# The output projection's second half of the last four tiles in a second PSUM bank, and five dead probability rows lent to the gathers of U

## What is computed

```
def diff_attention(q, k, v, lam, lambda_init, subln_g):
    ...
        p = jax.nn.softmax(sc, axis=-1)
        w = p[:, :, 0] - lam * p[:, :, 1]
...
        mix = jnp.einsum('bsk,kd->bsd', jnp.concatenate([att, ssd], axis=-1), w_out[l])
        x = layer_norm(alpha * x + mix, ln1_g[l], ln1_b[l])
        ffn = peer_ffn(x, peer_wq[l], peer_keys[l], peer_u[l], peer_v[l])
        x = layer_norm(alpha * x + ffn, ln2_g[l], ln2_b[l])
...
    def apply(args):
        hx, idx, g = args
        act = jax.nn.gelu(jnp.einsum('td,tkd->tk', hx, u_tab[idx]), approximate=False) * g
        return jnp.einsum('tk,tkd->td', act, v_tab[idx])
```

## Time and profile before

| | us |
|---|---|
| median of 3 executions | 3350.33 (3341.79, 3350.33, 3350.97) |
| the profiled execution, its own time | 3342.97 |
| its span in the profile | 3341.0 |
| PE busy | 2794.2 (84%) |
| DVE busy | 1888.3 (57%) |
| POOL busy | 1495.0 (45%) |
| ACT busy | 596.5 (18%) |

### The profile page before, as it was taken

The page is one execution under the profiler, slowest core; times in us unless marked ns, Lnnn a source line. Parts: engine busy times, 40 slices in busy tenths (PEclk is TensorE's granted clock), DMA queues, the critical chain, the costliest instruction groups (busy, mean ns, idle before and its releaser), DMA issues.

```text
span 3341.0 us, 32682 instructions
## 1 busy us (share of the span) xinstructions
PE 2794.2 (84%) x10171; PEld 1378.1 (41%) x10171; DVE 1888.3 (57%) x4634; ACT 596.5 (18%) x1288; POOL 1495.0 (45%) x1348
## 2 busy tenths in 40 slices
PE   8999979654255888747679999999999999999996
PEld 3455445432122555524334444444444444444442
DVE  3335444787589778768855555545565544445113
ACT  1321143221002778700000000100000000000000
POOL 0010011344444433444475566666666566665552
PEclk9999979887577989778889999999999999999998
DMA  3000021455688999899899999999999999999995
GB/s 129 28 26 26 26 81 60 142 173 177 214 309 284 349 375 384 326 373 336 315 386 388 402 398 398 370 406 389 404 403 379 377 398 396 406 396 381 367 371 204
DMA packets 307579, 981.57 MB, mean 294 GB/s; under 512 B 29904, under 2 KB 57680, under 8 KB 306640
## 3 DMA queue, kind: packets, MB, share of 16 engines
q0 software_dynamic: 184320, 671.17, 52.8%
q1 hardware_dynamic: 120464, 307.85, 24.4%
q10 hardware_dynamic: 2624, 0.46, 0.1%
HBM read 941.63 MB, written 37.75 MB: 293 GB/s over the span
## 4 chain that ended last, share of the span: by engine, by line
PE 28%; issue 13%; POOL 12%; DMA 9%; DVE 4%; ACT 3%; ACTq 1%; DVEq 0%; another core or an unknown queue 0%; POOLq 0%
PE part L1771 9%; PE hid L1752 8%; POOL u_ring L1690 8%; DMA v_ring<-in_peer_v_dram,ids_t 7%; PE acc L1809 6%; POOL v_ring L1704 4%; PE turn_ps L1744 4%; DVE u_ring L2087 2%; ACT dense_sums L1849 1%; PE part L1780 1%; DMA u_ring<-in_peer_u_dram,ids_u 1%; ACTq L1850 1%; ACT dense_sums L1851 1%; DMA room<-in_peer_v_dram 1%; ACT room L1897 1%
## 5 line engine op out<-in xcount | busy, mean ns | idle before, releaser
L2087 DVE CUSTOM_DVE_ANT_0 u_ring<-u_ring,x_rows_in 128x1024 f32<-128x1024 f32 x560 | 676.4, 1223 | 510.9 <-DMA u_ring<-in_peer_u_dram,ids_u 458.1
L1690 POOL DMA_INDIRECT u_ring<-in_peer_u_dram,ids_u x560 | 640.7, 1144 | 480.1 <-DVE dots L2087 328.9
L1704 POOL DMA_INDIRECT v_ring<-in_peer_v_dram,ids_t x560 | 595.4, 1063 | 484.9 <-PE acc L1809 318.2
L1771 PE MATMUL part<-room 128*128 128x512 f32 x1536 | 692.9, 601 | 87.9 <-DVE room L2063 77.5
L1752 PE MATMUL hid<-x1t_dense,room 128*128 128x384 f32 x2048 | 699.4, 495 | 4.6 <-DMA room<-in_peer_ut_dram 3.1
L1752 PEld LDWEIGHTS hid<-x1t_dense,room 128*128 128x128 f32 x2048 | 385.3, 192 | 338.1 <-issue 100.4
L1771 PEld LDWEIGHTS part<-room 128*128 128x128 f32 x1536 | 291.8, 192 | 447.8 <-issue 337.5
L1809 PE MATMUL acc<-v_ring,line 128*32 128x512 f32 x2240 | 296.2, 650 | 68.5 <-DMA v_ring<-in_peer_v_dram,ids_t 64.1
L1887 ACT ACTIVATE room<-hid 128x384 f32<-128x384 f32 x128 | 62.8, 491 | 1462.0 <-PE hid L1752 1224.4
L2073 DVE TENSOR_TENSOR dense_sums<-dense_sums,part 128x512 f32<-128x512 f32 x186 | 125.5, 684 | 262.9 <-PE part L1771 230.0
L412 PE MATMUL bank<-w_ring,xt 128*128 128x512 f32 x512 | 226.8, 596 | 2.6 <-issue 2.6
(11 more groups left out here) (318 smaller groups left out, 2657.2 us busy)
## 6 DMA issues: line engine op xcount, KB each, us to landing
wq_pair<-in_peer_wq_dram SPq DMA_DIRECT2D x32, 2048.0 KB
room<-in_peer_ut_dram SPq DMA_DIRECT2D x128, 512.0 KB
room<-in_peer_v_dram SPq DMA_DIRECT2D x128, 512.0 KB
gate_grid<-room SPq DMA_DIRECT2D x6, 4096.0 KB, 13.8
room<-gate_grid SPq DMA_DIRECT2D x32, 768.0 KB
w_ring<-in_w_in_dram SPq DMA_DIRECT2D x5, 2048.0 KB, 7.9
u_ring<-in_peer_u_dram,ids_u POOLq DMA_INDIRECT x560
v_ring<-in_peer_v_dram,ids_t POOLq DMA_INDIRECT x560
```

The costliest lines, as they stand in the source:

```text
L1690: pool.indirect_dma_start(u_ring[:, n % U_RING, :], None, peer_u, bass.IndirectOffsetOnAxis(ap=ids_u[:, q, k:k + 1], axis=0))\
L1704: pool.indirect_dma_start(row, None, peer_v, bass.IndirectOffsetOnAxis(ap=ids_t[:, q % 2, token:token + 1], axis=0))\
L1771: last = mm.matmul(part[k % 3][:], weights[:, n % 2, i, d * P:(d + 1) * P], vd[:, slot, half * 512:(half + 1) * 512], start=(i == 0), stop ...
L2087: vec.tensor_tensor_reduce(u_ring[:, n % U_RING, :], u_ring[:, n % U_RING, :], x1[:, q % 2, :], 1.0, 0.0, ALU.mult, ALU.add, dots[:, q % 2 ...
```

## The change

Two edits. The second half of the output projection of tiles t = 4 to 7 is accumulated in `TP[1]` instead of `OP`, and its bank is claimed and released through `t_free[1]` instead of `op_free`. And from k = `SPARE_FROM` = 48 on the gathers of U go round a ring of nine rows: the three rows of `probs0`, the two of `probs1` and the four of `u_rows`. Five new semaphores say that they landed; `spare_free`, given by ACT once it has seen the last item transposed (step 33), lets POOL issue k = 48 to 52. At step 33 POOL issues the gathers of steps 34 and 35, and later always those of two steps ahead. Eight semaphores of the scan and `spare_free` are released at the end of `build_mixer`, so that other numbers are handed out in `build_experts`.

```diff
+        SPARE_FROM = 4 * (items + 2 - CHOICE - 7)
+
+        def second_bank(t):
+
+            return TP[1] if t >= 4 else OP
...
+        def row_at(k):
+
+            if k < SPARE_FROM:
+                return u_rows[:, k % U_FIRST_RING, :]
+            i = (k - SPARE_FROM) % 9
+            return probs0[:, i, :] if i < 3 else probs1[:, i - 3, :] if i < 5 else u_rows[:, i - 5, :]
...
+        def rows_asked(n):
+
+            if n <= items:
+                return products(n + 1)
+            return [k for i in ((n + 1, n + 2) if n == items + 1 else (n + 2,)) for k in products(i)]
...
-                    for k in products(n + 1):
+                    for k in rows_asked(n):
                         if k % TOPK == 0:
                             pool.wait_ge(ids_ready, 1).then_inc(ids_ready, -1)
-                        pool.wait_ge(rows_free, 1).then_inc(rows_free, -1)
-                        pool.indirect_dma_start(u_rows[:, k % U_FIRST_RING, :], None, peer_u,
+                        if SPARE_FROM <= k < SPARE_FROM + 5:
+                            pool.wait_ge(spare_free, 1).then_inc(spare_free, -1)
+                        else:
+                            pool.wait_ge(rows_free, 1).then_inc(rows_free, -1)
+                        pool.indirect_dma_start(row_at(k), None, peer_u,
...
+                            elif half and t >= 4:
+                                pe.wait_ge(t_free[1], 1).then_inc(t_free[1], -1)
                             else:
                                 pe.wait_ge(op_free, 1).then_inc(op_free, -1)
+                            out = second_bank(t) if half else OP
                             for c in range(KC):
-                                last = mm.matmul(OP[:], mix_t[:, c, :], w_ring[:, half, c, :],
+                                last = mm.matmul(out[:], mix_t[:, c, :], w_ring[:, half, c, :],
...
+                        if m == items - 1:
+                            act.sem_inc(spare_free, 5)
...
-                            vec.scalar_tensor_tensor(out=part, in0=part, scalar=ALPHA, in1=OP[:],
+                            out = second_bank(t) if half else OP
+                            vec.scalar_tensor_tensor(out=part, in0=part, scalar=ALPHA, in1=out[:],
                                                      op0=ALU.mult, op1=ALU.add)
-                            dve.drain().then_inc(op_free, 1)
+                            dve.drain().then_inc(t_free[1] if half and t >= 4 else op_free, 1)
```

More of the change, by code:

```diff
@@ L209, in build_mixer @@
         xbc_smooth = sem("xbc_smooth")
-        dt_by_heads = sem("dt_by_heads")
-        dt_copied = sem("dt_copied")
-        dt_done = sem("dt_done")
+        dt_by_heads = handshake("dt_by_heads")
+        dt_copied = handshake("dt_copied")
+        dt_done = handshake("dt_done")
         xbc_ready = sem("xbc_ready")
@@ L215, in build_mixer @@
         conv_free = sem("conv_free")
-        turns_ready = sem("turns_ready")
+        turns_ready = handshake("turns_ready")
         trig_ready = sem("trig_ready")
-        lam_ready = sem("lam_ready")
-        lam_exped = sem("lam_exped")
+        lam_ready = handshake("lam_ready")
+        lam_exped = handshake("lam_exped")
         roped_ready = sem("roped_ready")
@@ L761, in build_mixer @@
         rows_landed = [sem(f"rows_landed{i}") for i in range(U_FIRST_RING)]
+        rows_landed += [sem(f"spare_landed{i}") for i in range(5)]
+        spare_free = handshake("spare_free")
         rows_free = sem("rows_free")
@@ L826, in products, with landed @@
             return range(min(done, FIRST_SLOTS), min(done + count(n), FIRST_SLOTS))
+        def row_at(k):
[3 more added lines that the diff above has]
+            return probs0[:, i, :] if i < 3 else probs1[:, i - 3, :] if i < 5 else u_rows[:, i - 5, :]
+        def landed(k):
+            if k < SPARE_FROM:
+                return k % U_FIRST_RING
+            return (U_FIRST_RING + (k - SPARE_FROM) % 9) if (k - SPARE_FROM) % 9 < 5 else (k - SPARE_FROM) % 9 - 5
+        def rows_asked(n):
+            if n <= items:
+                return products(n + 1)
+            return [k for i in ((n + 1, n + 2) if n == items + 1 else (n + 2,)) for k in products(i)]
         def tail(n, lag):
@@ L889, in _ @@
                             pool.tensor_copy(x1_first[:], tile).then_inc(x1_first_ready, 1)
-                    for k in products(n + 1):
+                    for k in rows_asked(n):
                         if k % TOPK == 0:
                             pool.wait_ge(ids_ready, 1).then_inc(ids_ready, -1)
-                        pool.wait_ge(rows_free, 1).then_inc(rows_free, -1)
-                        pool.indirect_dma_start(u_rows[:, k % U_FIRST_RING, :], None, peer_u,
+                        if SPARE_FROM <= k < SPARE_FROM + 5:
[3 more added lines that the diff above has]
+                        pool.indirect_dma_start(row_at(k), None, peer_u,
                                                 bass.IndirectOffsetOnAxis(ap=ids_first[:, k:k + 1], axis=0))\
-                            .then_inc(rows_landed[k % U_FIRST_RING], 16)
+                            .then_inc(rows_landed[landed(k)], 16)
             @block.tensor
@@ L1138, in _ @@
                             dve.wait_ge(x1_first_ready, 1)
-                        slot = k % U_FIRST_RING
-                        dve.wait_ge(rows_landed[slot], (k // U_FIRST_RING + 1) * 16)
-                        vec.tensor_tensor_reduce(u_rows[:, slot, :], u_rows[:, slot, :], x1_first[:], 1.0, 0.0, ALU.mult, ALU.add,
+                        row = row_at(k)
+                        dve.wait_ge(rows_landed[landed(k)], 16 * sum(landed(i) == landed(k) for i in range(k + 1)))
+                        vec.tensor_tensor_reduce(row, row, x1_first[:], 1.0, 0.0, ALU.mult, ALU.add,
                                                  dots_first[:, k:k + 1]).then_inc(rows_free, 1)
```

## The result

The changed kernel took 3316.65 us (median of four executions, 3300.18 to 3319.16) against 3350.01 before: ratio 0.9897, 95% interval 0.9876 to 0.9917. Its profiled execution took 3315.28 with a span of 3313.3, against 3341.0 before; that is 27.7 us less, with 30.5 foretold.

The account below looks back on a forecast made before the run. The attention block's last stretch was taken as a chain of waits with no engine full. 28.4 + 2.1 = 30.5 us gave 3312.5 or 3319.8, so 3316 was forecast; range 3308 to 3324 (71%).

Parts of the forecast that it names:

- Steps 26 and 30: Output projection: PE's waits of 1.09 and 1.02 us between the halves go with the second bank, saving 2.1 us.
- Step 34: Projection's second half follows the first without pause; DVE's second addition starts at 819.2 instead of 827.70, saving 8.5 us.
- The first round of gathers: k = 48 to 55 are issued by about 820, so rows for steps 34 and 35 land before DVE asks.
- POOL is not held at `spare_free`: ACT's last copy fulfils the wait with 17 us of cover; the rival that POOL is held had 1%.
- To the last tile's projection: Work on x1, transposes and `att` move up; the last projection starts at 842.2, 9.5 us earlier.
- the 0 for POOL's port: DVE dot products beside POOL's work on x1 could delay L884 by 0 to 2.3 us; the sum took 0.
- Step 38, the halves back to back: Last projection takes 9.49 + 7.11 us, DVE waiting about 7; 19.6 us saved up to here, step 34's 8.5 included.
- Steps 38 to 41: 10.3 us from second addition to step 39 unchanged; last twelve dot products end about 883.7, 28.4 us earlier.
- The tail keeps its pace: Rival, 15%: DMA engines limit the gathers, twelve dot products again take 23 us; gain 21.7 us, time 3321 to 3329.
- Lost behind the barrier: Rival, 8%: the expert part meets its transfers in another phase and loses 20 to 30 us; time 3333 to 3355.
- slower by the clock: Rival, 4%: PE's granted clock in the expert part is 0.02 lower, losing 40 us; time 3355 to 3365.
- Two levels of the time of before: Four executions before were read as two levels, the timed median 7.4 us above the profiled one; forecast set between them.

## Why the prediction was right, step by step

I had 3316 us, and 3316.65 was measured. The mechanism held; the sum was short by 2.3 in the block (30.5 for 32.8), and the agreement to 1 us of the median is luck, since the four executions lie between 3300.18 and 3319.16 and the expert part alone scatters by 8.

- *Steps 26 and 30*, 2.1: 1.8 by the kernel that takes just these back, 1.7 between the kernel before (793.84 - 683.55 = 110.3) and the changed one (108.6). Right but for the clock at step 30: the waits went, and the matmuls took 16.45 us in place of 8.80 + 7.11.
- *Step 34*, 8.5: the additions are 10.08 - 1.41 = 8.7 us nearer. Right.
- *The first round of gathers; POOL is not held at `spare_free`.* Right. POOL issues `probs` behind the last `u_rows` with no wait of its own, 17 us after ACT's last copy:

```profile
807.41 0.94 POOL L923 DMA_INDIRECT u_rows<-in_peer_u_dram,ids_first  x1 [0.31 <-issue]
808.65 0.94 POOL L923 DMA_INDIRECT probs<-in_peer_u_dram,ids_first  x1 [0.30 <-issue]
```

- *To the last tile's projection*, 48.4 us from the start of step 34's: 48.0 (843.07 - 795.10). Right, the 0 for POOL's port included, though the meeting did take place: one dot product was stretched to 3.35 us, and the four instructions on `att` from 1.13 to 3.20. It was DVE that stood still, not POOL. POOL's two operations on x1 took as long as before from the first's start to the second's end, 5.7 us and 5.6:

```profile
831.81 2.44 POOL L908 TENSOR_TENSOR x<-x,g 128x1024 f32<-128x1024 f32 x1
834.43 3.10 POOL L910 TENSOR_TENSOR x<-x,b 128x1024 f32<-128x1024 f32 x1 [0.18 <-POOLq L909]
```

`att` was done at 838.46, ahead of the 840.01 at which PE came to it. Before, two instructions of DVE met them too, the dot product of 3.92 us in the earlier trace rows and this one:

```profile
842.83 3.35 DVE L1141 CUSTOM_DVE_ANT_0 u_rows<-u_rows,x_first 128x1024 f32<-128x1024 f32 x1
```

- *Step 38, the halves back to back, 9.49 + 7.11*: mis-sized. They took 13.97, so from DVE's first addition to its second it was 5.05 us, 3.56 of them idle, and not 7. The first half did not begin at the low level of the clock. The prediction's rule, that halves after no or 1 us of idle PE take 7.1 us, does not fit its own rows either: the half of 9.49 us stood only 1.12 behind the transposes. It moved the 9.49 over unchanged. The stretches before and in the first half, in the kernel before and in the changed one (columns as in the earlier trace rows; the seventh is the granted clock as a share of 2.4 GHz):

```profile
847.00:851.70 4.70, 2.62 (x12) 1.85 (x10) 1.38 (x6) 2.35 (x4) 3.78 (x4) 0.50 0.65 190
851.76:856.50 4.74, 4.74 (x6) 2.14 (x7) 1.23 (x2) 0.00 (x0) 1.14 (x2) 0.50 1.00 379
```

```profile
839.00:843.00 4.00, 2.92 (x13) 2.01 (x11) 4.00 (x7) 2.39 (x4) 3.39 (x3) 0.58 0.83 260
843.07:850.00 6.93, 6.93 (x16) 3.12 (x17) 2.96 (x7) 0.00 (x0) 5.42 (x5) 1.00 0.97 341
```

Before, PE stood 1.02 us between the transposes of x1 and those of `att` and began the projection at 1.2 GHz; after, `att` is there in time, the transposes follow each other, and the clock is at 2.4 GHz from the projection's first matmul. These 2.6 us are what the sum lacks; the other terms together are 0.3 to 0.4 too high. In all four traces with a gap of about 1 us there, the first half took the longer time (9.49 and 9.22 alone, 15.68 and 16.60 for both halves); of nine without it, eight took 7 us a half, and one 15.92 for both. No kernel changed the gap alone, so that the gap decides is argued, not shown.
- *Steps 38 to 41*: from the second addition to step 39 10.3 foretold and 10.34 measured; twelve dot products 14.4, measured 14.7. Right; 23.3 in the kernel with the bank alone shows that it is the gathers' edit that does it.
- *The tail keeps its pace* (first rival): no. The DMA engines could give more: from 829 to 859 us they move 294 GB/s now, and from 829 to 879 us, the stretch of the earlier trace rows with its 200, they move 287.

```profile
829.00:859.00 30.00, 17.86 (x48) 9.00 (x48) 21.95 (x33) 2.39 (x4) 21.58 (x17) 0.78 0.79 294
```

- *Lost behind the barrier, or slower by the clock*: no. The expert part's PE clock (0.92 before; 0.93 and 0.92 in two executions of the changed kernel) and length are those of before to within the scatter. My test for it, 5 us, was too narrow: one and the same program differs by more.
- *Two levels of the time of before.* I took four executions for two levels, 3342 and 3350. The 36 later ones lie anywhere from 3335.68 to 3359.51. No two levels are to be seen in them; the place between was a fair guess for a poor reason.
- *The range.* Its low end holds 3 us for waits of POOL for which no row was given. No run shows them; what the block gained beyond the sum was the clock of step 38.

## What to carry to other kernels

Where two engines hand one buffer to and fro, look at which is late, not only at how long the wait is: the 17.5 us that PE stood at step 34 were worth 8.5, and at step 38 either of two edits could remove most of one wait, so that alone they gave 19.5 and 19.0 and together 32.8. More buffers for a gather are worth only a part until the queue that issues it also runs further ahead of its other waits: with nine rows and one step ahead the block stayed 7 us above the changed kernel's, of the 13 us that the gathers add to the bank. When a part of the program that is not touched scatters by more than the effect, measure the effect between two events in the trace; here the block of the changed kernel repeated to 0.2 us in three traces, while its 15 executions lay between 3300.18 and 3319.16.

## What was not expected of the hardware

The 32 matmuls of step 38, behind the same instructions, took 13.97, 15.68, 15.92 or 16.60 us in different kernels; those of 15.68 and more had a granted clock of 0.50 in their first 1.6 us, and those of 13.97 had 1.00. Wherever there was a pause of 1 us in the short work ahead, they took the longer times; without it one kernel of nine did. The Trainium skill (TensorE: Matmul & The Clock Gate, "What's actually happening") says that the clock gate knows just two levels and that when it lifts varies from run to run of one kernel; the traces agree: the kernel with seven dot products at step 37 took 16.46 us for the halves of step 30 in one execution and 15.67 in another.
